# The third group of the convolutional feed-forward part works by seven block products too; left and right outputs change places

## What is computed

```python
def conv_ffn(h, w_up, conv_w, conv_b, w_down):
    u = h @ w_up
    up = jnp.pad(u, ((0, 0), (1, 1), (0, 0)))
    u = up[:, :-2] * conv_w[0] + up[:, 1:-1] * conv_w[1] + up[:, 2:] * conv_w[2] + conv_b
    g, val = u[..., :D_FF], u[..., D_FF:]
    return (jax.nn.silu(g) * val) @ w_down

x = x + conv_ffn(rms_norm(x, norm2_g[l]), w_up[l], conv_w[l], conv_b[l], w_down[l])
return rms_norm(x, final_norm_g)
```

## Time and profile before

| | us |
|---|---|
| median of 3 runs | 2036.19 |
| lowest and highest | 2035.24, 2038.74 |
| the profiled execution, its own time | 2036.41 |
| its span | 2034.0 |
| second group's seven products (1890.4 to 1929.4) | 39.0 |
| third group's up blocks (1929.4 to 1994.7) | 65.3 |
| third group's down product (1994.7 to 2027.5) | 32.8 |
| from the last matmul's end to the end of the span | 6.5 |

### The profile page before, as it was taken

How to read it: one execution, slowest core, us unless ns; L and a number is a source line. 1 busy time by engine, 2 the same in 40 slices (tenths; PEclk the granted TensorE clock), 3 DMA queues, 4 the chain that set the end, 5 groups by cost and what they waited for, 6 DMA issues and landing times.

```text
span 2034.0 us, 26973 instructions
## 1 busy us (share of the span) xinstructions
PE 1994.4 (98%) x10702; PEld 1665.4 (82%) x10702; DVE 1300.2 (64%) x1764; ACT 921.7 (45%) x1315; POOL 146.4 (7%) x136
## 2 busy tenths in 40 slices
PE   6999999999999999999999999999999999999998
PEld 5898888888877888988888888877777798888887
DVE  4668867576765555855685735346679746766855
ACT  3333475445436222356454446245455545434433
POOL 0000010000001025110000001000111000000000
PEclk9999999999999999999999999999999999999999
DMA  9563346475764623624754542410132124252421
GB/s 321 166 236 96 117 166 185 142 227 130 225 219 147 205 85 103 195 83 127 225 143 126 140 145 94 122 48 25 48 117 79 50 94 130 68 175 83 124 94 72
DMA packets 203567, 273.58 MB, mean 134 GB/s; under 512 B 11298, under 2 KB 162237, under 8 KB 202037
## 3 DMA queue, kind: packets, MB, share of 16 engines
q1 hardware_dynamic: 174272, 215.03, 32.7%
q0 software_dynamic: 13888, 37.75, 7.9%
q10 hardware_dynamic: 15285, 19.10, 2.9%
HBM read 258.60 MB, written 12.62 MB: 133 GB/s over the span
## 4 chain that ended last, share of the span: by engine, by line
PE 86%; DVE 6%; DMA 3%; ACT 2%; DVEq 2%; issue 1%; SPq 0%; ACTq 0%; POOL 0%; POOLq 0%
PE bank L829 17%; PE bank L902 14%; PE bank L1306 11%; PE bank L1288 11%; PE bank L1612 5%; PE bank L1006 4%; PE bank L1522 4%; PE bank L1631 3%; PE bank L1076 2%; PE bank L1494 1%; PE bank L1505 1%; PE bank L1220 1%; PE bank L933 1%; DMA ada_half<-in_ada_w 1%; PE bank L1469 1%
## 5 line engine op out<-in xcount | busy, mean ns | idle before, releaser
L2888 DVE TENSOR_TENSOR w_both_lo<-raw,w_both_hi 128x2048 fp32r<-128x2048 f32 x40 | 91.6, 2289 | 51.6 <-ACT w_both_hi L1974 51.4
L829 PE MATMUL bank<-h_hi,w_both_hi 128*128 128x512 f32 x304 | 120.5, 396 | 0.0
L829 PE MATMUL bank<-h_lo,w_both_hi 128*128 128x512 f32 x304 | 119.4, 393 | 0.0
L829 PE MATMUL bank<-h_hi,w_both_lo 128*128 128x512 f32 x304 | 119.3, 392 | 0.0
L1974 ACT ACTIVATE w_both_hi<-raw 128x2048 fp32r<-128x2048 f32 x40 | 76.2, 1908 | 51.9 <-PE bank L1306 34.2
L2398 DVE TENSOR_TENSOR w_both_lo<-raw,w_both_hi 128x2048 fp32r<-128x2048 f32 x29 | 67.3, 2321 | 40.1 <-ACT w_both_hi L1660 39.7
L2479 DVE TENSOR_TENSOR w_both_lo<-raw,w_both_hi 128x2048 fp32r<-128x2048 f32 x32 | 73.3, 2289 | 26.3 <-ACT w_both_hi L1686 25.5
L1306 PE MATMUL bank<-w_both_hi,a_hi 128*128 128x512 f32 x224 | 87.1, 389 | 0.0
L1306 PE MATMUL bank<-w_both_lo,a_hi 128*128 128x512 f32 x224 | 87.1, 389 | 0.0
L1306 PE MATMUL bank<-w_both_hi,a_lo 128*128 128x512 f32 x224 | 87.1, 389 | 0.0
L2293 ACT ACTIVATE tmp<-bank,vcols 128x512 f32<-128x512 f32 x44 | 34.0, 778 | 102.8 <-PE bank L1612 68.9
(11 more groups left out here) (568 smaller groups left out, 6070.6 us busy)
## 6 DMA issues: line engine op xcount, KB each, us to landing
...
```

The lines of the kernel that those rows point to most:

```text
L829: mm = pe.matmul(o, x, y, start=(k == 0 and j == 0), stop=(k == kc - 1 and j == 2))
L2888: dve.tensor_tensor(lo, f_raw[fast_raw(g, name)][:], f32(hi), ALU.subtract).then_inc(sem("f_lo"), 1)
```

## The change

Group 2 becomes a group like the others, with 6 blocks: halves of k are 3 wide, so the right quarters are 128 by 1536 (`conv_w`, `conv_raw`) and the left ones 128 by 768. `CONV_FAST`, `tile` and `tok_pair` are gone from this part. Core of the diff:

```diff
-CONV_FAST = 2
+CONV_RAW = [dict(zip(names, [0, 1, 2, 0, 1, 2, 0, 1, 2, 0, 1, 1] if g < 2 else [0, 1, 2, 0, 1, 2, 0, 1, 2, 3]))
+            for g, names in enumerate(CONV_NAMES)]
+CONV_ORDER = 2 * [[0, 1, 2, 3, 4, 5, 6]] + [[0, 1, 2, 3, 5, 4, 6]]
...
+    order = [x for x in CONV_ORDER[g] if x != 5 or g == 2]
+    return 76 + 12 * g + 2 * order.index(m) + c + 1
...
+        c_raw = f_raw + [at("raw3", "AD", [P, TILE])]
...
+        def conv_part(g, name):
+            kh, n0 = CONV[g][1] // 2, 512 if name[2] == "1" else 0
+            return conv_rows(g)[:, kh * (name[1] == "2"):kh * (name[1] == "2") + kh, n0:n0 + 512]
...
@@ TensorE
-                for ks in (((0, 1), (2, 3)) if m == 1 else ((0, 1, 2, 3),)):
+                for ks in ((range(kh - 2), range(kh - 2, kh)) if m == 1 else (range(kh),)):
...
-            for n in range(nb):
-                tile(t0 + 2 + n, n % 2, q0 + n // 2, h_hi, h_lo, parts=slot(CONV_LAST[n // 2], n % 2),
-                     added=conv_added(CONV_FAST - 1, 6, 0) if n == 0 else None)
-            tok_pair(t0 + 2 + nb, q0 + 3, CONV_LAST[-2], g_hi, g_lo, kc=nb, ready=(sem("conv_g"), 2), groups=((0, 1), (2,), (3,)))
-            tok_pair(t0 + 4 + nb, q0 + 4, CONV_LAST[-1], g_hi, g_lo, kc=nb)
+                for m in CONV_ORDER[g]:
+                    conv_product(g, m)
@@ VectorE, up part
-                    if n == 6:
-                        conv_sum(cs_sum[:, 0:2], quarter(1, 0)[:, 0:2], quarter(1, 1)[:, 0:2], ALU.subtract)
-                    if n == 7:
+                    if n == nb - 2:
+                        conv_sum(cs_sum[:, some], a21[:, some], a22[:, some], ALU.subtract)
+                    if n == nb - 1:
                         conv_w_sum(g, "B22")
@@ VectorE, behind the products: (group, product, first token block, column half, sign)
-                conv_add(g, 0, 0, 0, ALU.add)
+                conv_add(g, 0, 0, 1, ALU.add)
...
-                conv_add(g, 1, 2, 1, ALU.add)
+                conv_add(g, 1, 2, 0, ALU.add)
...
@@ VectorE, the end
+            for c in range(2):
+                x_gained(c, 0)
+            for c in range(2):
+                conv_add(2, 5, 0, 1, ALU.add, (c,))
+                x_summed(c)
+            for c in range(2):
+                left_squared(c)
+            x_all(0)
+            conv_add(2, 4, 2, 0, ALU.subtract, (0,))
+            x_all(1)
+            conv_add(2, 4, 2, 0, ALU.subtract, (1,))
+            dve.drain()
+            for c in (2, 3):
+                x_gained(c, 0)
+            scale_left(0)
+            scale_left(1)
+            conv_add(2, 6, 2, 1, ALU.add, (0,))
+            x_summed(2)
+            for c in (2, 3):
+                left_squared(c)
+            x_all(2)
+            conv_add(2, 6, 2, 1, ALU.add, (1,))
+            x_summed(3)
+            scale_left(2)
+            x_all(3)
+            scale_left(3)
```

More of the change, by code:

```diff
@@ L3304, in conv_w_sum, with conv_add @@
                 dve.wait_ge(sem(which), n)
-                to = f_raw[CONV_RAW["B11"]][:]
-                conv_sum(to, to, f_raw[CONV_RAW[more]][:], ALU.add)
-            def conv_add(g, m, row, part, op):
-                for c in range(2):
+                conv_sum(conv_raw(g, "B11"), conv_raw(g, "B11"), conv_raw(g, more), ALU.add)
+            def conv_add(g, m, row, part, op, cs=(0, 1)):
+                for c in cs:
                     dve.wait_ge(sem("f_product"), conv_made(g, m, c))
```

327 lines of the change are left out of this document (151 added, 176 removed).

## The result

The changed kernel takes 2039.75 us (median of 20 runs, 2036.93 to 2041.76), the kernel before 2036.91 us (20 runs, 2032.76 to 2041.51): **1.0014 of before, 95% interval 1.0008 to 1.0020**, 2.8 us more. The interval leaves out 1.000, so the change costs something, but less than the 0.2% that the forecast set as the bound of "no change". Forecast were 2038.9 us and 0.63 for "within 0.2%". 18 matmuls are gone and nothing is won.

The account below looks back on a forecast made before the run. TensorE bounds the old kernel; in the changed third group VectorE's queue would make it wait. From 2036.2 us, -4.1 matmuls, +5.3 waits and +1.5 tail give +2.7 and 2038.9 us, range 2034.0 to 2042.0.

Parts of the forecast that it names:

- within 0.2%: Whole kernel: change of at most 0.2%, 4.1 us, either way, not told from no change; chance 0.63.
- 18 matmuls fewer, 4.1 us: Third group's down product: 126 matmuls for 144, -4.1 us on TensorE's path if nothing waits.
- The exchange, group two, the transfers of w_down: nothing: First two groups: left and right exchanged, two additions fewer in group two, larger w_down loads issued early; no time change.
- The new widths by the line through three rows: VectorE remainders 1536 and 768 wide, in group three: 1.755 and 0.955 us, from the line through 512, 1024 and 2048.
- The starts of the products: Third group's down product: TensorE waits 0.3, 1.5, 0.7, 0.2 and 2.6 us on VectorE's queue, 5.3 us in all.
- rival 2: Product 6: clock falls behind the 2.6 us wait; 0.8 us more, 2039.7, or 3.2 more, 2042.1; chance 0.3 of over 0.2% slower.
- a granted clock of 0.50 in product 6: Third group's product 6: halved TensorE clock there, named as a sign that the forecast was wrong.
- It decides once product 6 takes over 5.5 us: Third group's last product: length above which the slower clock decides; 1.4 us more of chain waits was the other condition.
- The tail: After the last matmul: VectorE's remaining additions, gains and scalings, then 4.1 us for the output; +1.5 us.
- more than 6.5: Kernel's end: over 6.5 us from the last matmul to the end, as a sign of being right.
- The sum: Third group's down product to the end: -4.1 matmuls, +5.3 waits, +1.5 tail, together +2.7 us.
- over 90% busy in the 37 us behind T: VectorE in the 37 us from the third group's first product: over 90% busy, as a sign of being right.

Follow-up runs that it names:

- e3: Changed kernel with ten extra matmuls in TensorE's wait before product 6, into a bank nobody reads; 1.0001 of before (0.9992 to 1.0009).
- e1: Kernel before, with only left and right outputs exchanged in the first two groups, third group as before; 0.9999 of before (0.9990 to 1.0007).
- e4: Changed kernel with the last row block's variance ahead of the scaling of row block 2's left half on VectorE; 1.0012 of before (1.0003 to 1.0020).
- e2: Changed kernel with product 4's two additions on VectorE moved ahead of product 5's; 1.0004 of before (0.9995 to 1.0012).
- e5: e2 with two VectorE gains done a second time behind the gains of row blocks 2 and 3; 1.0018 of before (1.0009 to 1.0027).
- e11: e10 with product 0's first addition moved into an idle gap of VectorE; 1.0004 of before (0.9995 to 1.0014).
- e10: e9 with gain and scaling of each left half fused into one VectorE operation, row blocks' steps interleaved; 1.0003 of before (0.9994 to 1.0012).
- e9: e2 with VectorE's steps behind the last addition reordered to scaling, last variance, gain; 1.0009 of before (1.0000 to 1.0018).

## Why the prediction was right

- **18 matmuls fewer, 4.1 us.** Right in count (10684 for 10702). As a gain in time it did not arrive: e3 put ten back, in a wait, for nothing.
- **The exchange, group two, the transfers of w_down: nothing.** Right (39.2 and 39.0 us for the two groups in e1 and in the changed kernel; no wait of TensorE on a transfer behind T).
- **The new widths by the line through three rows.** 1.755 and 0.955 taken, 1.754 and 0.955 measured.
- **The starts of the products.** Forecast T + 9.95, 14.75, 19.05, 23.1 and 29.8 for products 2, 3, 5, 4 and 6; measured 9.95, 14.73, 19.06, 23.24 and 29.80. (The profile's waits of 1.26 and 2.32 us count from the modelled end of the matmul before; from the time at which the next one was due they are 1.4 and 2.5, for 1.5 and 2.6.) The walk along VectorE's queue, operation by operation, was worth its length.
- **The clock.** It was kept out of the forecast and stood as rival 2, with two sizes. It did fall, for 3.6 us, and with it one of the prediction's own signs of being wrong came true, "a granted clock of 0.50 in product 6". TensorE's last matmul ends at T + 35.8 where the rival said 35.7, and the price is 0.94 us (e3) where it said 0.8. This is the step that was mis-set: the term stood at nothing. The trace of before does not settle which case was the likelier, though it holds more than the earlier trace rows. Stretches of it, at the start and in a phase with a second fall, then TensorE's timeline ahead of that fall:

```profile
20.00:22.00 2.00, 1.92 (x33) 1.18 (x33) 2.00 (x2) 0.00 (x0) 0.00 (x0) 1.00 1.10 348
22.00:24.00 2.00, 1.85 (x13) 1.29 (x10) 0.35 (x2) 1.62 (x2) 0.00 (x0) 1.00 1.10 348
...
1298.00:1300.00 2.00, 2.00 (x6) 1.61 (x5) 0.96 (x2) 0.00 (x0) 1.01 (x1) 0.50 0.00 0
...
1293.98 1.84 PE L886 MATMUL bank<-ones,tmp 128*128 128x1 f32 x16
1295.68 1.44 PE L1414 MATMUL bank<-ones,tmp 128*128 128x1 f32 x8
```

A wait of 2.34 us that ended at 20.08 left the clock at 1.00 over the next 4 us, one of 3.05 us that ended at 26.91 was followed by 0.50, and about 1296 the clock fell behind no wait of 1 us at all but behind 24 matmuls one column wide. In the earlier trace rows it fell within the wait, in product 6 only 1.35 us behind it. So the length of a wait alone does not say when the clock falls. In e4 the fall behind product 6's wait (2.30 us) came again, with the same late end.
- **A sum in rival 2.** "It decides once product 6 takes over 5.5 us" does not come out: from a start at T + 29.8 to VectorE's T + 34.9 there are 5.1 us, from which it costs anything, and the verdict (1.4 us more) turns at 6.5. It took 5.97, so it cost and did not turn the verdict.
- **The tail.** Last addition forecast at T + 34.9, and at T + 34.93 where the clock is kept (e2, e3). Output 4.1 us behind the power, measured 3.9. 6.9 us lie between the last matmul's end and the span's, for "more than 6.5".
- **The sum.** T + 42.0 forecast, 41.7 without the clock's fall, 42.65 with it: +2.7 forecast, +3.3 by T in the profiles, +2.8 in the medians. That +2.8 stands so close to +2.7 is in part luck: the clock added 0.94 us that the forecast had at nothing, while the tail came out 0.3 us shorter and the time outside the span 0.45 us shorter than it was reckoned. In microseconds the result lies 0.85 above the forecast; 0.7 of that is before's own median, 2036.91 over 20 runs where the forecast stood on 2036.19 over 3. For the same reason it is no proof of rival 2 that 2039.75 equals its first figure, 2039.7.
- **VectorE's queue is the bound in these 40 us.** Forecast over 90% busy in the 37 us behind T: 33.8 of 37.0. Shown from both sides: TensorE 4.2 us earlier moves the end 0.9 (e2), VectorE 1.4 us longer moves it 1.4 (e5), 0.6 us less moves it 0.6 (e11). It is a queue with waits in it and not volume alone: 2.1 us less ahead of a wait moved the last addition 0.84 (e10), and the two output transfers are a bound close behind (e4, e9).
